# Two projection stages that open on other conditions, one weight load issued ahead, and a head preparation with its means taken inside the root

## What is computed

```python
def rmsnorm_2(x, g):
    xf = x.astype(jnp.float32)
    y = xf * lax.rsqrt(jnp.mean(xf * xf, axis=-1, keepdims=True) + RMS_EPS)
    return (y * g.astype(jnp.float32)).astype(x.dtype)

# even layer: 3328 projected columns; 26 heads of 64 are normalised, 10 of them rotated
qa, ka, va, qb, kb, vb, gate = _split(h @ w_in, SPLIT_E)
qa = rmsnorm_2(qa.reshape(B, S, H_A, D_HEAD), gq_a)
...
qb = jnp.concatenate([rotate(qb[..., :half], ang_row), rotate(qb[..., half:], ang_col)], -1)

# odd layer: 2976 projected columns, two "latents" of 256 and 128 that are projected again;
# 16 heads of 96 and 16 of 64 are normalised and partly rotated
cq, ckv, kpe, qd, kd, vd, gate = _split(h @ w_in, SPLIT_O)
q = (rmsnorm_2(cq, g_cq) @ w_cq_b).reshape(B, S, H_C, C_NOPE + C_ROPE)
kv = (rmsnorm_2(ckv, g_ckv) @ w_ckv_b).reshape(B, S, H_C, C_NOPE + C_V)
...
qc = rmsnorm_2(q, gq_c)
```

## Time and profile before

| | us |
|---|---|
| median of 3 runs | 3354.15 (3349.62 to 3358.97) |
| the profiled execution | 3350.66 |
| its span in the trace | 3349.0 |
| TensorE busy | 3020.6 |
| VectorE busy | 1673.3 |
| ScalarE busy | 1161.2 |
| GpSimd busy | 969.7 |

### The profile page before, as it was taken

One profiled execution on the slowest core, in us unless ns is written; L12 is line 12 of the kernel. 1 busy time (PEld: TensorE's weight loads), 2 busy tenths in 40 slices (PEclk: granted clock), 3 DMA queues, 4 the chain that ended last, 5 costly groups with the idle time before them and its releaser, 6 DMA issues.

```text
span 3349.0 us, 51559 instructions
## 1 busy us (share of the span) xinstructions
PE 3020.6 (90%) x18916; PEld 2641.7 (79%) x18916; DVE 1673.3 (50%) x3183; ACT 1161.2 (35%) x2131; POOL 969.7 (29%) x627
## 2 busy tenths in 40 slices
PE   5898986999999999997989999978697889999969
PEld 4587954777888888787989769968695889988869
DVE  2699724614233231322056568861203948778871
ACT  2311136423222211312122457740321327667640
POOL 1122111252222235552235023311222543433211
PEclk9899997999999999998999999989898999999989
DMA  2222131331111114332386342311225761231311
GB/s 99 59 94 103 70 107 40 106 113 60 47 50 50 44 50 132 113 126 95 108 204 196 90 97 59 120 76 50 82 92 198 200 175 51 62 77 39 125 76 50
DMA packets 220499, 317.24 MB, mean 95 GB/s; under 512 B 80742, under 2 KB 166630, under 8 KB 217142
## 3 DMA queue, kind: packets, MB, share of 16 engines
q1 hardware_dynamic: 185190, 268.90, 26.9%
q10 hardware_dynamic: 33360, 39.98, 3.4%
q0 software_dynamic: 1792, 6.29, 0.6%
HBM read 221.56 MB, written 93.57 MB: 94 GB/s over the span
## 4 chain that ended last, share of the span: by engine, by line
PE 69%; DVE 8%; ACT 3%; issue 2%; DMA 1%; POOL 1%; SPq 0%; POOLq 0%; DVEq 0%; ACTq 0%; PEldq 0%
PE psum L506 15%; PE psum L2268 14%; PE psum L2471 7%; PE psum L1083 6%; PE psum L1052 6%; PE psum L2222 6%; PE psum L1063 5%; PE psum L767 2%; PE psum L744 2%; PE psum L2019 2%; DVE arena L2858 2%; PE psum L756 1%; DVE arena L2842 1%; PE psum L1098 1%; PE psum L3187 1%
## 5 line engine op out<-in xcount | busy, mean ns | idle before, releaser
L2268 PE MATMUL psum<-parts_ffn 128*128 128x512 f32 x2112 | 482.2, 391 | 3.6 <-DVE parts_ffn L2169 3.6
L2268 PEld LDWEIGHTS psum<-parts_ffn 128*128 128x128 f32 x2112 | 398.3, 189 | 87.2 <-issue 2.2
L506 PE MATMUL psum<-parts_even,parts_ffn 128*128 128x256 f32 x2496 | 307.1, 286 | 28.2 <-ACTq L534 26.0
L506 PEld LDWEIGHTS psum<-parts_even,parts_ffn 128*128 128x128 f32 x2496 | 304.9, 195 | 29.0 <-issue 26.5
L506 PE MATMUL psum<-parts_odd 128*128 128x248 f32 x2304 | 278.1, 283 | 35.7 <-ACT arena L544 16.2
L506 PEld LDWEIGHTS psum<-parts_odd 128*128 128x128 f32 x2304 | 273.7, 193 | 39.4 <-ACT arena L544 18.8
L2338 DVE SCALAR_TENSOR_TENSOR arena<-psum,arena 128x1023 f32<-128x1023 f32 x88 | 112.9, 1283 | 328.2 <-ACT arena L2322 322.0
L544 ACT ACTIVATE arena<-psum 128x256 f32<-128x256 f32 (+1 forms) x232 | 87.1, 382 | 474.2 <-PE psum L506 469.5
L435 PE MATMUL psum<-parts_mixer 128*128 128x512 f32 x912 | 211.0, 394 | 11.0 <-ACTq L444 11.0
L435 PEld LDWEIGHTS psum<-parts_mixer 128*128 128x128 f32 x912 | 173.8, 191 | 48.5 <-ACTq L444 7.6
L1125 ACT ACTIVATE both<-psum 128x512 fp32r<-128x512 f32 x256 | 140.0, 596 | 107.4 <-PE psum L1063 107.0
(11 more groups left out here) (345 smaller groups left out, 5871.7 us busy)
## 6 DMA issues: line engine op xcount, KB each, us to landing
arena<-ffn_up_b SPq DMA_DIRECT2D x44, 512.0 KB, 3.3
arena<-ffn_down_k SPq DMA_DIRECT2D x44, 512.0 KB, 3.6
arena<-x SPq DMA_DIRECT2D x10, 2048.0 KB, 8.9
arena<-w_in_e SPq DMA_DIRECT2D x13, 1024.0 KB, 6.3
e_tokens<-arena ACTq DMA_DIRECT2D x26, 512.0 KB, 3.3
arena<-w_in_o SPq DMA_DIRECT2D x12, 992.0 KB, 5.8
o_tokens<-arena ACTq DMA_DIRECT2D x24, 496.0 KB, 3.0
arena<-w_in_f SPq DMA_DIRECT2D x19, 512.0 KB, 3.4
```

The source lines that it names most:

```text
L506: last = pe.matmul(self.bank(t), self.hT[:, a, k, t * P:(t + 1) * P], self.weights.parts[:, self.weights.slot(s), b, k, :], start=(k, a, b ...
L2268: last = pe.matmul(self.core.psum[:, 4 * u + 2 * s + h, :], parts[:, s, a, k, :], self.hT[:, b, k, h * HALF:(h + 1) * HALF], start=(k, a, ...
```

## The change

1. `open_next` on ACT in `down` moves from the end of the first half's work to just ahead of `part(0, 0)`. The wait for `after` moves out of `start_scalar` into `scalar`, so that the opening alone no longer waits.
2. `tok3b` opens after `first.taken_out` (`tok3a`'s last take-out from PSUM) in place of `first.done` (its last stores have landed).
3. In `ProjectAndPrepare`, ACT does the take-outs of the units 0 to 3 ahead of square(0) and root(0).
4. On SP `load_first` of `tok4b` stands ahead of `latents` in place of behind it.
5. DVE's four small instructions for the means are gone. ACT's root now divides and adds the constant itself (`scale`, `bias`), with one instruction for each run of heads of one width: one in `prep3`, two in `prep4`. POOL sets the constant once (`clear`).
6. `prep4` gets `scalar_alone`: ACT takes out all 6 groups of a tile, DVE none.

```diff
     def start_scalar(self, act):
-        hold(act, self.after)
         act.sem_inc(self.act_out, len(self.banks))
...
     def scalar(self, act):
+        hold(act, self.after)
         if not self.opened_before:
...
         def part(act, h, k):
+            if (h, k) == (0, 0):
+                self.open_next(act)
             source, high, _ = self.parts_of(h, k)
...
         self.order(act, self.high, drain, finish, part)
-        self.open_next(act)
         for k in range(KT):
...
-        self.A, self.B = (self.G + 1) // 2, self.G // 2
+        self.A, self.B = (self.G, 0) if scalar_alone else ((self.G + 1) // 2, self.G // 2)
+        self.roots = []
+        for at, head, count, d, _ in self.parts():
+            if self.roots and self.roots[-1][2] == d:
+                self.roots[-1][1] = head + count
+            else:
+                self.roots.append([head, head + count, d])
...
     def root(self, act, n):
-        act.wait_ge(self.mean_ready, n + 1)
-        act.activation(self.ss[:, n % 2], self.ss[:, n % 2], ACT.Sqrt).then_inc(self.rooted, 1)
+        act.wait_ge(self.reduced, len(self.segments) * (n + 1))
+        if n == 0:
+            act.wait_ge(self.eps_set, 1)
+        for a, b, d in self.roots:
+            act.activation(self.ss[:, n % 2, a:b], self.ss[:, n % 2, a:b], ACT.Sqrt, scale=1.0 / d, bias=self.eps).then_inc(self.rooted, 1)
+
+    def clear(self, pool):
+        hold(pool, self.after[0] + self.after[TT - 1] + self.scalar_after)
+        pool.memset(self.eps, EPS).then_inc(self.eps_set, 1)
...
-        for g in range(first_group, self.G, 2):
+        for g in range(first_group, self.G, 1 if self.scalar_alone else 2):
...
-        dve.wait_ge(self.reduced, S_ * (n + 1))
-        for at, head, count, d, _ in self.parts():
-            part = self.ss[:, n % 2, head:head + count]
-            last = dve.tensor_scalar(part, part, 1.0 / d, EPS, ALU.mult, ALU.add)
-        last.then_inc(self.mean_ready, 1)
...
         project, prep = self.project, self.prep
+        hold(act, project.after)
         project.start_scalar(act)
-        for n in range(self.steps):
+        for unit in self.units(0):
+            project.take_out(act, *unit)
+        prep.square(act, 0)
+        prep.root(act, 0)
+        for n in range(1, self.steps):
...
-        rest = ProjectTokens(core, "tok3b", a["w_in_e"][7:13], hT, e_tok[:, 1792:3328], 6, 256, first.done,
+        rest = ProjectTokens(core, "tok3b", a["w_in_e"][7:13], hT, e_tok[:, 1792:3328], 6, 256, first.taken_out,
...
+        add(Part(sync=rest.weights.load_first))
         add(latents)
-        add(Part(sync=rest.weights.load_first))
```

More of the change, by code:

```diff
@@ L2747, in __init__ @@
         self.xs, self.sq = core.take(R, self.width), core.take(2, self.width)
-        self.ss = core.take(2, self.heads)
+        self.ss, self.eps = core.take(2, self.heads), core.take(1)
         self.sines = core.take(2, sum(r[1] * 2 * r[4] * r[5] for r in ropes))
@@ L2938, in gpsimd @@
         for n in range(self.steps):
+            if n == 1:
+                prep.clear(pool)
             if 0 <= n - 1 < TT:
@@ L3605, in build @@
                         [(0, 96, 8, qc), (768, 96, 8, kc), (1536, 128, 8, dd)],
-                        [first.done + latents.turned_out + latents.stored_tile(n) for n in range(TT)], stage_slots=1)
+                        [first.done + latents.turned_out + latents.stored_tile(n) for n in range(TT)], stage_slots=1, scalar_alone=True)
         prep.scalar_after, prep.later_after = latents.done, latents.done
```

20 lines of the change are left out of this document (12 added, 8 removed).

## The result

| | us |
|---|---|
| kernel before, median of 4 runs | 3354.68 (3349.62 to 3358.97) |
| changed kernel, median of 4 runs | 3322.6 (3318.79 to 3324.29) |
| ratio, 95% interval | 0.9903 (0.9886 to 0.9921) |
| changed kernel, the profiled execution | 3324.29, span 3322.7 |

The median lies 0.6 us from the predicted 3322.0, and inside the range. Run again on another chip (five runs beside nine of the kernel before), the changed kernel took 3323.18 us and the kernel before 3346.80: 0.9930 (0.9916 to 0.9943). So the gain is 32 us by the first comparison and 24 by the second; the forecast was 29.8. The changed kernel took the same time in both; what differs is the kernel before, 3354.68 and 3346.80 us.

What follows compares the result with a forecast made beforehand. TensorE, busy 3020.6 of 3349.0 us, was taken as the bound, so gains lie in its waits: 5.0 + 6.4 + 18.4 = 29.8 us off gives 3320.9, placed a little higher at 3322; range 3309 to 3337.

Steps and rivals of the forecast that it cites:

- Place A: tok3a's start (item 1): PE does units 0 and 1 inside its wait; 5.0 us gained, ends 4.8 and 6.5.
- Place B: tok3b's start (items 2, 3, 5): PE no longer waits for the last store; 6.4 us gained, ends 4 and 9.
- The first square: tok3b: behind units 0 to 3, a take-out and a DMA issue, it starts at 1709.6, 1.55 us later.
- The root's table load: tok3b: 1.28 us behind the sums instead of beside them; tile 0's multiplication ends 0.2 us later.
- The rotated tile 4: tok3b: ready 3.4 us earlier; with 3.0 us to spare, PE can be earlier by 6.4 us and no more.
- Place C: tok4b and prep4 (items 3 to 6): earlier start 11.9 us plus DVE's chain; 18.4 us gained, ends 13 and 24.
- Odd tiles: tok4b, DVE's chain: 14.44 us become 12.2; gain 2.3 each in tiles 3 and 5, 0.9 in tile 1.
- the even tiles' 0: tok4b, tiles 2, 4, 6: the multiplication waits for POOL's split to end, so 18.3 us stay; gain 0.
- ACT's extra take-outs: tok4b (item 6): three more a tile at 0.5 us and one more root, 1.7 us; costed at nothing.
- The fuller gain: Rival, whole change: POOL's CAST doesn't hold L2858, gains add up more fully; about 39 us off, 3312; chance 0.19.
- nothing was given back in sum: Rival, whole change: head preparation gives back the earlier start's gain; about 22 us off, 3330; chance 0.17.
- The stage slot on ACT: Rival, tok4b: ACT's take-outs wait for the previous tile's store; 27 us lost, 3354 or above; chance 0.06.

Runs made afterwards that it cites:

- e3: The changed kernel with item 4 undone: tok4b's first two weight blocks load behind the latents' stores again; 3336.07 us, ratio 0.9964 to the kernel before.
- e5: The changed kernel with item 5 undone: DVE makes the means in four small instructions, ACT takes one root; 3324.48 us, ratio 0.9929 to the kernel before.
- e6: The changed kernel with item 3 undone in both stages: first square and root around unit 0's take-out again; 3315.47 us, ratio 0.9906 to the kernel before.
- e9: The changed kernel with item 3 undone in both stages and item 4 undone; 3326.30 us, ratio 0.9939 to the kernel before.
- e11: The changed kernel, split off GpSimd, step 1's root in tok4b behind all take-outs, step 2's first unit ahead of the first turn; 3314.44 us, ratio 0.9898.
- r0: The changed kernel unaltered, run again on the follow-up runs' chip; 3323.18 us, ratio 0.9930 to the kernel before.
- e7: The changed kernel with the CAST of tok4b's blocks 2 to 5 on ScalarE, subtraction still on GpSimd; 3316.85 us, ratio 0.9908 to the kernel before.
- e8: The changed kernel with tok4b's split of blocks 2 to 5 off GpSimd: CAST on ScalarE, subtraction on VectorE; 3314.36 us, ratio 0.9898 to the kernel before.
- e1: The changed kernel with item 1 undone: tok3a opens at the end of the first half's work; 3325.11 us, ratio 0.9937 to the kernel before.
- e2: The changed kernel with item 2 undone: tok3b opens when tok3a's last stores have landed; 3331.58 us, ratio 0.9954 to the kernel before.

## Why the prediction was right, and where its terms were off

**The total** was forecast at 3322 and measured at 3322.60. That it came within 0.6 us is partly luck. The places brought 2.1 us more than the 29.8, stretches outside them took 5.7 us back, and the median lies 1.7 us below the profiled execution, where the forecast put it 1.1 above. The profiled execution alone was forecast at 3320.9 and took 3324.29. The mechanism of each place is borne out by the runs that undo it.

**Place A** was 5.0 and measured 4.9, in the profile and by undoing it. The signs came as forecast: first product at 1513, unit 4 at 1538.66, slow transposes. The wait after 48 products was 4.25 us and not some 5, since those products took 8.13 us and not 7.48. In five of the other traces (e3, e5, e6, e9, e11) the units 2 and 3 ran slowly too, and unit 4 stood 29.6 us behind the transposes in place of 28.2; by the opening of `tok3b` all of them but e6 had made that up.

**Place B** was 6.4 and measured 8.0 in the first profile and 10.6 in r0, which is above the text's own upper end of 9. The first square was put 1.55 us later than before, and came so (1705.08, plus the 4.59 that A had brought, is 1709.67). Two steps were off. The root's table load was put behind DVE's sums; it ran beside them, since the table is loaded ahead of the root's own wait. Tile 0's multiplication so ended 1.2 us earlier and not 0.2 later. And the tiles behind it gained more. From tile 0 to tile 4 the ends of the multiplication lie 51.0 us apart and lay 56.7 apart, a gain of 5.7 where 3.6 were counted: 1.2 of the difference in the tiles 2 and 4, which were to gain nothing, and 0.9 in 1 and 3. The rotated tile 4 so came some 7 us earlier in place of 3.4, and PE's turn of it no longer bounds the stage: 2.4 us are left. What bounds it is tile 0's turn, for which the text gave 7.9. Beyond place A it came 9.4 us earlier in the first profile, with 1.6 given back by the clock behind it, and 10.3 in r0, with nothing given back. The text has no term for the clock there. The drain of 1.38 us that the Trainium skill counts beside a table load ("ScalarE: Activation LUTs", section "What ACT_TABLE_LOAD costs") doesn't show behind either load here: the Exp follows at 1692.30, when the load's 1.28 us from 1691.01 are over, and the root stands 0.83 us behind its load, waiting for DVE.

**Place C** was 18.4 and measured 19.0. Its start was 11.9 (11.5 measured), the chain behind it 6.5 (7.8: 115.7 us from the first square to the last root before, 107.9 after). Odd tiles were to be 12.2 and are 12.4; even ones were to stay, at 18.3, and fell to 17.6: GpSimd's rotation ahead of the split took 1.7 us in place of 2.0, and the multiplication ended 6.2 us behind the split in tile 4, where it had ended 6.7 behind it. That GpSimd's split holds DVE there, on which the even tiles' 0 rests, is shown by e7 and e8. What the prediction did not say is what its parts are worth alone: the start rests on item 4, which costs 16.1 us if it alone is undone, and item 3, counted as part of the gain, costs 1.8 us at PE's last products in `tok4b` with early weights and 4.8 with late ones.

**The items without a price.** ACT's extra take-outs in `tok4b` did cost nothing: none of them waits for a store in the changed kernel, where with item 6 undone (e4) ACT waited four times, for 7.7 us in all. In `tok3b`, which keeps its shared take-outs, one tile's wait for a store took 2.23 us, and PE did not stand for it. In item 3 I saw only what it asks of the square (1.55 us). Where the loads landed about 10 us behind the opening (e6, e9) it was no condition of the opening on take-outs: with four banks PE could have gone on for 11.7 us.

**The rivals.** The fuller gain did not come, because the CAST and the subtraction hold the multiplication. Inside the places nothing was given back in sum, though the clock took 1.6 us in place B. The stage slot on ACT didn't turn. Outside the places the profiled pair lost 5.7 us, and I did not count that. In thirteen traces of changed kernels the stretch from the near attention to `tok4a` takes 519.5 to 521.7 us, against 519.22 in the one of the kernel before, and that from the `diff` attention to the end 596.4 to 600.8 against 595.72. Whether the earlier start does this or the one trace is a favourable one stays open; no run here tells it apart.

## What to carry to other kernels

- Price each part of a change with the others in place, and once without: item 3 looked like a condition of items 2 and 4, and was a loss beside both in the executions that were traced.
- If two engines' chains alternate between long and short steps, look at what the third engine does in the long one. Here GpSimd's 6.4 us of splitting every second tile held VectorE, and moving it to ScalarE (1.85 us) and VectorE (2.21 us) gave more at the last root (9.5 us) than the means and the take-outs together (5.6).
- When an order is to be turned round, don't take the landing of a load from one trace. The tile's loads landed 13.7 us behind the opening in one execution and 10.0 in another, and by the first of them e6 was forecast slower where it was faster.

## What the runs showed of the hardware that was not expected

- An increment of a semaphore on ACT, queued behind a table load and an Exp, took effect while the table was loading and before the Exp had run (load from 1691.01 to 1692.29, PE's products from 1691.34, the Exp at 1692.30).
- The subtraction of 128x1984 takes 4.53 us on GpSimd and 2.21 on VectorE, which it holds up for 4.2 us while it runs on GpSimd.
- After a pause of 3.18 us at the same place of the program PE went on at a granted clock of 1.00 in r0, e3 and e4, and in e1 at 0.89 over the next 14.6 us, which cost 1.6 us. The length of the pause alone doesn't tell which it will be.
- The same store of 512 KB landed 7.1 us after its issue in one execution (e2), 12.6 in another (the kernel before) and 15.4 in a third (the changed kernel's first profile).
